# The diagonal of a gated recurrence as two added matmul groups instead of one on the sum of the keys

## The chip, the cores and the metric

The kernel runs on one core of a Trainium2 chip. The metric is the time of one execution on the device in microseconds (us). Below, TensorE is PE, VectorE DVE, ScalarE ACT, GpSimd POOL, and SyncE, which here only issues transfers, SP.

## The reference, cut to what matters

Two transformer blocks run one after the other on 256 tokens of width 2048. Everything here is in the first block, in its recurrent half: eight heads of a bidirectional gated recurrence (HGRN2), with 128 keys per head.

```python
def _hgrn2_direction(q, f_logit, v, lb):
    f = lb + (1.0 - lb) * jax.nn.sigmoid(f_logit)
    return _gla_chunkwise(q, 1.0 - f, v, jnp.log(f))    # the key is k = 1 - f
...
    # in _gla_chunkwise: S_t = diag(f_t) S_{t-1} + k_t v_t^T ; o_t = S_t^T q_t
    a = jnp.einsum('bhtd,bhsd,bhtsd->bhts', q_, k_, jnp.exp(rel))   # rel = b_t - b_s, s <= t
...
    o_fwd = _hgrn2_direction(q, ff, v, lb_fwd)
    o_bwd = jnp.flip(_hgrn2_direction(jnp.flip(q, 1), jnp.flip(fb, 1), jnp.flip(v, 1), lb_bwd), 1)
    o = _rmsnorm(o_fwd + o_bwd, norm_g)
```

At s = t the decay is exp(0) = 1. The diagonal of the summed forward and backward matrix is therefore q·kf + q·kb, which is also q·(kf + kb).

## The kernel before, in words

The kernel is written by hand, with its own semaphores. Each engine follows one list of instructions in order. The list is built from **phases**; a phase is a row of weight chunks of 512 KB. Each chunk goes through four slots: SP loads it into `w_raw` (L663), ACT rounds it to `w_hi` (L1270, L1267), DVE forms the remainder `w_lo` = `w_raw` - `w_hi` (L1742), and PE multiplies both with the activations. SP loads a chunk into a slot once the remainder of the chunk four before it is formed. ACT rounds a chunk once PE has used the chunk four before it. A finished panel of four chunks is moved out of PSUM by an ACT copy (L1291) and a DVE add (L1846).

All other work hangs on the chunks by number: the function `beside` of each engine says what it does after chunk j of a phase. Among it are the pieces of the modulation matrix `w_mod` (512 KB each, loaded by SP at L673, multiplied on DVE at L1809 and L1812).

The phases that matter are, in order:

- `in_f`, 48 chunks: forget gates forward and backward (`hf`, `hb`) and queries (`hq`). Beside them run the attention heads, and the keys `kf` = 1 - `hf`, `kb` = 1 - `hb` on DVE after chunks 37 and 42 (L2313). After chunk 44 DVE forms `qb` = `kf` + `kb` (L2317), which uses the buffer of the later backward queries.
- `in_hg`, 16 chunks, and `w_oa`, 32 smaller ones: beside them runs the recurrence, `hgrn_step(g)`, with g counting the chunks of `in_hg` and on through `w_oa`.

The recurrence is worked out in levels. After chunk 2 of `in_hg` PE runs `diagonal()` (L1097): for each of the 8 heads and 2 halves, four 32x32 blocks of keys times queries, 128 matmuls in all, into PSUM bank 4. It waits for the last panel of `in_f` (the queries), for `mods_done` to reach 8, and for the sum of the keys. `mods_done` reaches 8 by `take_mods(6, 5)` (L2201), the first thing that DVE does in its `hgrn_step(4)`. ACT copies bank 4 to `a_near` (L1626); the entries off the diagonal are replaced later by the levels.

DVE then waits for `diagonal()` and forms `qb` = `hq`·`hb` (L2324) and `hq` = `hq`·`hf` in place (L2326). The first level needs both. Ten steps follow, two (forward, backward) for each of the levels 1, 2, 4, 8 and 16: PE runs 128 matmuls (L1146) after chunks 4 to 13; DVE, after chunks 7 to 16, takes the result with a predicated copy (L2373) and updates queries, keys and gates (L2388, L2391, L2395). A PE step waits for the DVE update of the level before. Two wide levels (L1159), the part off the diagonal (L1170) and the outputs (L1179) follow in `w_oa`.

The matmuls of `diagonal()` and of the levels are small, and PE gets two instructions for each: a weight load and a matmul. In the last level steps and between them nothing loops: the list is unrolled.

Of the kernel before, what the change touches and what calls it, by code (L numbers as in the profile page):

```python
# [21 lines left out]
ALU = mybir.AluOpType  # L22
# [3 lines left out]
P = 128  # L26
# [55 lines left out]
STRIP = 32  # L82
STRIPS = P // STRIP
# [109 lines left out]
def build(nc, d, out):  # L193
    ctx = ExitStack()
    with ctx:
# [52 lines left out]
        ps = ctx.enter_context(nc.psum_tensor("ps", [P, 8, 512], F32))  # L248
# [25 lines left out]
        kf = place("kf", [P, HEADS, T], F32, big + 16 * size_tile)  # L274
        kb = place("kb", [P, HEADS, T], F32, big + 24 * size_tile)
        v1_tok = place("v1_tok", [P, 2, HEADS, P], F32, big + 32 * size_tile)
        qb = place("qb", [P, HEADS, T], F32, big + 32 * size_tile)
        hb = place("hb", [P, HEADS, T], F32, big + 40 * size_tile)
# [314 lines left out]
        def added_at(o, half, quarter):  # L593
# [6 lines left out]
        x_loads = sem("x_loads")  # L600
        late_loads = sem("late_loads")
        c_sig, c_silu = map(sem, ("c_sig", "c_silu"))
        lb_diff, lb_sig, f_sig, lb_done, f_done, k_done, ksum_done, q_done = map(
            sem, ("lb_diff", "lb_sig", "f_sig", "lb_done", "f_done", "k_done", "ksum_done", "q_done"))
        diag_mm, diag_moved = map(sem, ("diag_mm", "diag_moved"))
        ho_stat, ln_stat = Count(sem("ho_stat")), Count(sem("ln_stat"))
        level_mm, level_selected, level_updated, level_placed, off_mm, off_moved = map(
# [147 lines left out]
        def _(pe):  # L755
# [341 lines left out]
            def diagonal():  # L1097
                pe.wait_ge(summed, summed_all("in_f"))
                pe.wait_ge(mods_done, 8)
                pe.wait_ge(ksum_done, 1)  # L1100
                for u in range(2 * HEADS):
                    h, half = divmod(u, 2)
                    for strip in range(STRIPS):
                        cut = slice(half * P + strip * STRIP, half * P + (strip + 1) * STRIP)
                        mm = pe.matmul(ps[strip * STRIP:(strip + 1) * STRIP, 4, u * STRIP:(u + 1) * STRIP],
                                       qb[:, h, cut], hq[:, h, cut], start=True, stop=True)
                mm.then_inc(diag_mm, 1)

            def hgrn_step(g):
# [616 lines left out]
        def _(dve):  # L1726
# [467 lines left out]
            def take_mods(before, bank):  # L2194

                dve.wait_ge(mod_mm, before + 2)
                at_ = 8 * before
                turned = ps[:, bank, :].rearrange("p (i j s) -> p j i s", j=STRIPS, s=STRIP)[:, :, :, 0]
                to, less = (c.rearrange("p (j i) -> p j i", j=STRIPS)
                            for c in (mods[:, at_:at_ + DT], column("b_mod", at_, DT)))  # L2200
                dve.tensor_tensor(to, turned, less, ALU.add).then_inc(mods_done, 2)  # L2201
                dve.wait_ge(mods_done, before + 2)
# [94 lines left out]
            def forget_step(j):  # L2297

                if j == 29:
                    for i, name in enumerate(("hgrn_lb_logits_fwd", "hgrn_lb_logits_bwd")):  # L2300
                        dve.tensor_tensor(lb[:, 2 * i, :], column(name, 0, HEADS), column(name, HEADS, HEADS),
                                          ALU.subtract).then_inc(lb_diff, 1)
                if j == 33:
                    dve.wait_ge(lb_sig, 2)
                    for i in range(2):
                        dve.tensor_scalar(lb[:, 2 * i + 1, :], lb[:, 2 * i, :], -1.0, 1.0, ALU.mult,
                                          ALU.add).then_inc(lb_done, 1)
                if j in (37, 42):
                    i = (37, 42).index(j)
                    if i == 0:  # L2310
                        dve.wait_ge(*att1.out(HEADS))
                    dve.wait_ge(f_done, HEADS * (i + 1))
                    dve.tensor_scalar((kf, kb)[i][:, :, :], (hf, hb)[i][:, :, :], -1.0, 1.0, ALU.mult,  # L2313
                                      ALU.add).then_inc(k_done, 1)
                if j == 44:
                    dve.wait_ge(k_done, 2)
                    dve.tensor_tensor(qb[:, :, :], kf[:, :, :], kb[:, :, :], ALU.add).then_inc(ksum_done, 1)  # L2317

            def hgrn_step(g):

                if g == 4:
                    take_mods(6, 5)
                    dve.wait_ge(diag_mm, 1)
                    dve.tensor_tensor(qb[:, :, :], hq[:, :, :], hb[:, :, :], ALU.mult).then_inc(q_done, 1)  # L2324
                    dve.wait_ge(q_done, 1)
                    dve.tensor_tensor(hq[:, :, :], hq[:, :, :], hf[:, :, :], ALU.mult).then_inc(q_done, 1)  # L2326
                    dve.wait_ge(q_done, 2)
                    dve.wait_ge(diag_moved, 1)
                if 7 <= g < 7 + N_STEPS:
                    level_step(g - 7)  # L2330
                if g in (18, 20):
                    dve.wait_ge(level_mm, N_STEPS + g // 2 - 8)
                    for way in range(2):
                        level_update(g - 8 + way)
                if g == 24:
                    dve.wait_ge(hg_sig, 1)
                    dve.tensor_tensor(hg[:, :, :], hg[:, :, :], hb[:, :, :], ALU.mult).then_inc(hg_gate, 1)
                if g == 26:
                    dve.wait_ge(ho_sum, 1)
                    dve.tensor_scalar(rstd[:, :], ps[:, 4, 0:T], 1.0 / P, EPS, ALU.mult, ALU.add  # L2340
                                      ).then_inc(ho_stat.sem, 1)
                    invert_root(rstd[:, :], ho_stat)
                if g == 29:
                    dve.wait_ge(hg_gate, 1)
                    for i in range(2):
                        heads, banks = slice(4 * i, 4 * i + 4), slice(4 + 2 * i, 6 + 2 * i)
                        dve.wait_ge(ho_sum, 2 + i)
                        dve.scalar_tensor_tensor(qb[:, heads, :], qb[:, heads, :], column("hgrn_norm_g"),
                                                 ps[:, banks, :].rearrange("p b (h t) -> p (b h) t", t=T),
                                                 ALU.mult, ALU.mult).then_inc(h_out, 1)  # L2350
                        dve.wait_ge(h_out, 2 * i + 1)
                        dve.tensor_tensor(qb[:, heads, :], qb[:, heads, :], hg[:, heads, :],
                                          ALU.mult).then_inc(h_out, 1)
                        dve.wait_ge(h_out, 2 * i + 2)
                if g in (30, 31):
                    i = g - 30
                    dve.wait_ge(h_hi, i + 1)
                    tiles = slice(HEADS + 4 * i, HEADS + 4 * i + 4)
                    dve.tensor_tensor(acts[:, tiles, 1, :], qb[:, 4 * i:4 * i + 4, :],
                                      acts[:, tiles, 0, :].bitcast(F32), ALU.subtract).then_inc(h_lo, 1)  # L2360
# [204 lines left out]
```

## Time and profile before

| what | us |
|---|---|
| median of 3 runs | 2661.23 (2660.72 to 2662.78) |
| the profiled execution, its own time | 2660.91 |
| its span in the profile | 2659.0 |
| granted clock of PE, mean over the span | 0.994 of full speed |

The rows in the section after next are from this profiled execution. Times in them count from the start of its span. A row of the timeline gives the start, the duration (of the group when "xN" stands behind it), the engine, the line, the operation with its tiles, and in brackets how long the engine sat idle before it and what ended that. "issue" there means that the engine waited for nothing that the profile shows. Starts and ends of neighbours on one engine overlap by about 0.1 us.

### The profile page before, as it was taken

What the parts mean: (1) busy time and instruction counts of PE and PEld (TensorE: products, weight loads), DVE (VectorE), ACT (ScalarE), POOL (GpSimd) and SP (SyncE); (2) the same over time, 40 slices, a digit from 0 to 9 for tenths busy, and PEclk for the clock granted to TensorE, in tenths of its full rate; (3) what the DMA queues carried; (4) which work ended last, traced back from release to release, by engine and by line L of the source; (5) the groups of instructions that cost most, each with busy time, mean ns of one, the idle gap of its engine ahead of it and who ended that gap; (6) DMA issues with size and microseconds to landing.
All of it is one profiled execution on the core that took longest, in us unless ns stands there. A gap on an engine that the chain in (4) does not pass through costs nothing.

```text
span 2659.0 us, 39728 instructions
## 1 busy us (share of the span) xinstructions
PE 2578.0 (97%) x15041; PEld 2168.5 (82%) x15041; DVE 1829.7 (69%) x2290; ACT 1216.9 (46%) x1562; POOL 58.4 (2%) x83
## 2 busy tenths in 40 slices
PE   6899999989999999999999999999999999999998
PEld 3588777868888888888888888878788888888887
DVE  5778899888864456645648888887666555555444
ACT  4354553464434344444544444465644444444343
POOL 2100000020000000000010000000000000000000
PEclk8999999999999999999999999999999999999999
DMA  9978794858866666565565655556466555566554
GB/s 359 362 256 306 233 344 161 299 185 293 282 206 226 195 188 186 188 197 184 175 212 179 199 175 167 167 180 201 150 198 189 189 187 186 187 189 207 194 193 158
DMA packets 413756, 567.09 MB, mean 213 GB/s; under 512 B 17997, under 2 KB 302066, under 8 KB 412736
## 3 DMA queue, kind: packets, MB, share of 16 engines
q1 hardware_dynamic: 408800, 548.72, 63.2%
q0 software_dynamic: 4832, 16.68, 1.8%
q8 instruction: 83, 1.36, 0.2%
q14 instruction: 41, 0.34, 0.0%
HBM read 563.22 MB, written 2.11 MB: 213 GB/s over the span
## 4 chain that ended last, share of the span: by engine, by line
PE 48%; DVE 2%; ACT 0%; issue 0%; DVEq 0%; ACTq 0%
PE ps L783 22%; PE ps L780 11%; PE ps L802 5%; PE ps L801 5%; PE ps L800 5%; DVE w_lo L1742 1%; PE ps L881 0%; PE ps L903 0%; DVE x_tok L2009 0%; DVE tmp L1849 0%; DVE pr L1829 0%; PE ps L837 0%; DVE ring L2159 0%; ACT pr L1708 0%; DVE pr L1856 0%
## 5 line engine op out<-in xcount | busy, mean ns | idle before, releaser
L1742 DVE TENSOR_TENSOR w_lo<-w_raw,w_hi 128x1024 fp32r<-128x1024 f32 (+1 forms) x870 | 1051.9, 1214 | 670.0 <-ACT w_hi L1267 347.6
L783 PE MATMUL ps<-acts,w_hi 128*128 128x512 f32 x4096 | 1321.7, 398 | 15.9 <-DVE w_lo L1742 7.8
L780 PEld LDWEIGHTS ps<-acts,w_lo 128*128 128x128 f32 x4096 | 769.9, 188 | 169.1 <-issue 1.2
L1270 ACT CAST w_hi<-w_raw 128x1024 fp32r<-128x1024 f32 (+1 forms) x542 | 563.7, 1044 | 647.5 <-PE ps L783 567.9
L780 PE MATMUL ps<-acts,w_lo 128*128 128x256 f32 x4096 | 828.4, 278 | 0.5 <-issue 0.5
L783 PEld LDWEIGHTS ps<-acts,w_hi 128*128 128x128 f32 x4096 | 640.2, 189 | 38.1 <-issue 15.2
L1267 ACT CAST w_hi<-w_raw 128x1024 fp32r<-128x1024 f32 x328 | 339.4, 1040 | 474.1 <-PE ps L802 393.5
L800 PE MATMUL ps<-w_hi,ff 128*128 128x512 f32 x864 | 336.3, 389 | 0.0
L802 PE MATMUL ps<-w_hi,ff 128*128 128x512 f32 x864 | 336.1, 389 | 0.0
L801 PE MATMUL ps<-w_lo,ff 128*128 128x512 f32 x864 | 336.1, 389 | 0.0
L800 PEld LDWEIGHTS ps<-w_hi,ff 128*128 128x128 f32 x864 | 162.2, 188 | 34.5 <-issue 0.8
L801 PEld LDWEIGHTS ps<-w_lo,ff 128*128 128x128 f32 x864 | 162.2, 188 | 33.9
L802 PEld LDWEIGHTS ps<-w_hi,ff 128*128 128x128 f32 x864 | 162.2, 188 | 33.3
L800 PE MATMUL ps<-w_hi,acts 128*128 128x512 f32 (+1 forms) x384 | 152.8, 398 | 4.4 <-DVE w_lo L1742 2.7
L1812 DVE SCALAR_TENSOR_TENSOR mod_acc<-mod_w,silu_c,mod_acc 128x1024 f32<-128x1024 f32 x120 | 151.9, 1277 | 0.0
L801 PE MATMUL ps<-w_lo,acts 128*128 128x512 f32 (+1 forms) x384 | 149.9, 390 | 0.0
L802 PE MATMUL ps<-w_hi,acts 128*128 128x512 f32 (+1 forms) x384 | 149.8, 390 | 0.0
L1829 DVE SCALAR_TENSOR_TENSOR pr<-pr,cols (+15 forms) x240 | 113.9, 475 | 10.9 <-DVE pr L1829 6.0
L1291 ACT COPY half_sum<-ps 128x512 f32<-128x512 f32 x154 | 89.6, 582 | 39.9 <-PE ps L783 39.9
L800 PEld LDWEIGHTS ps<-w_hi,acts 128*128 128x128 f32 x384 | 74.3, 193 | 29.9 <-issue 11.9
L802 PEld LDWEIGHTS ps<-w_hi,acts 128*128 128x128 f32 x384 | 74.2, 193 | 14.4
L801 PEld LDWEIGHTS ps<-w_lo,acts 128*128 128x128 f32 x384 | 74.4, 194 | 13.6
(331 smaller groups left out, 1542.1 us busy)
## 6 DMA issues: line engine op xcount, KB each, us to landing
w_raw<-in_w_in SPq DMA_DIRECT2D x216, 512.0 KB, 3.9
w_raw<-in_w_down SPq DMA_DIRECT2D x216, 512.0 KB, 4.5
w_raw<-in_w_gate_up SPq DMA_DIRECT2D x176, 512.0 KB, 3.6
mod_w<-in_w_mod SPq DMA_DIRECT2D x160, 512.0 KB, 6.3
w_raw<-in_w_up SPq DMA_DIRECT2D x128, 512.0 KB, 4.2
w_raw<-in_w_out SPq DMA_DIRECT2D x64, 512.0 KB, 4.7
mod_more<-in_w_mod SPq DMA_DIRECT2D x32, 512.0 KB, 12.0
w_raw<-in_w_in POOLq DMA_DIRECT2D x16, 512.0 KB, 7.2
```

What stands on the lines that cost most here:

```text
L780: mm = pe.matmul(ps[:, bank, 0:T], w_lo[:, slot, k, c:c + P], lin_.act[:, kk, 0, :], start=False, stop=at_last and n == 0, skip_group_chec ...
L783: mm = pe.matmul(ps[:, bank, :], w_hi[:, slot, k, c:c + P], lin_.act[:, kk, :, :], start=at_first, stop=at_last and n == 1, skip_group_che ...
L800: pe.matmul(o, a_hi, hi, start=at_first, stop=False, skip_group_check=True)
L801: pe.matmul(o, a_hi, lo, start=False, stop=False, skip_group_check=True)
L802: mm = pe.matmul(o, a_lo, hi, start=False, stop=at_last, skip_group_check=True)
L1267: act.copy(wide[1][:, slot, 0:kn, 0:lin_.width], wide[0][:, slot, 0:kn, 0:lin_.width]).then_inc(hi_ready, 1)
L1270: act.copy(w_hi[:, slot, 0:kn, 0:lin_.width], w_raw[:, slot, 0:kn, 0:lin_.width]).then_inc(hi_ready, 1)
L1291: act.copy(half_sum[:, pair, 0:n, :], ps[:, 2 * pair:2 * pair + n, T:2 * T]).then_inc(half_ready, 1)
L1742: dve.tensor_tensor(low[cut], raw[cut], high[cut].bitcast(F32), ALU.subtract).then_inc(lo_ready, 1)
L1812: ins = dve.scalar_tensor_tensor(acc, mod_w[:, slot, :], c, acc, ALU.mult, ALU.add)
L1829: ins = dve.scalar_tensor_tensor(o, z_, w, o, ALU.mult, ALU.add)
```

## The change

DVE's sum of the keys (L2317) and its semaphore go. PE forms the diagonal by two matmuls that add up in PSUM, of forward and of backward keys, so it runs 256 small matmuls instead of 128, and waits for the keys (`k_done`) instead of their sum. As `qb` no longer holds the sum, DVE forms the backward queries' product before it waits for `diagonal()`.

```diff
@@ diagonal(), PE
-                pe.wait_ge(ksum_done, 1)
+                pe.wait_ge(k_done, 2)
                 for u in range(2 * HEADS):
                     h, half = divmod(u, 2)
-                    for strip in range(STRIPS):
-                        cut = slice(half * P + strip * STRIP, half * P + (strip + 1) * STRIP)
-                        mm = pe.matmul(ps[strip * STRIP:(strip + 1) * STRIP, 4, u * STRIP:(u + 1) * STRIP],
-                                       qb[:, h, cut], hq[:, h, cut], start=True, stop=True)
+                    for way, k_ in enumerate((kf, kb)):
+                        for strip in range(STRIPS):
+                            cut = slice(half * P + strip * STRIP, half * P + (strip + 1) * STRIP)
+                            mm = pe.matmul(ps[strip * STRIP:(strip + 1) * STRIP, 4, u * STRIP:(u + 1) * STRIP],
+                                           k_[:, h, cut], hq[:, h, cut], start=way == 0, stop=way == 1,
+                                           skip_group_check=True)
                 mm.then_inc(diag_mm, 1)
@@ forget_step(j), DVE
-                if j == 44:
-                    dve.wait_ge(k_done, 2)
-                    dve.tensor_tensor(qb[:, :, :], kf[:, :, :], kb[:, :, :], ALU.add).then_inc(ksum_done, 1)
@@ hgrn_step(g), DVE
                 if g == 4:
                     take_mods(6, 5)
+                    dve.tensor_tensor(qb[:, :, :], hq[:, :, :], hb[:, :, :], ALU.mult).then_inc(q_done, 1)
                     dve.wait_ge(diag_mm, 1)
-                    dve.tensor_tensor(qb[:, :, :], hq[:, :, :], hb[:, :, :], ALU.mult).then_inc(q_done, 1)
-                    dve.wait_ge(q_done, 1)
                     dve.tensor_tensor(hq[:, :, :], hq[:, :, :], hf[:, :, :], ALU.mult).then_inc(q_done, 1)
                     dve.wait_ge(q_done, 2)
                     dve.wait_ge(diag_moved, 1)
```

## Rows read from the trace of the kernel before

**Rows 1.** The page: busy time by engine.
```profile
PE 2578.0 (97%) x15041; PEld 2168.5 (82%) x15041; DVE 1829.7 (69%) x2290; ACT 1216.9 (46%) x1562; POOL 58.4 (2%) x83
```
**Rows 2.** Busy time by window: PE, PEld, DVE, ACT, POOL, clock, DMA share, GB/s.
```profile
370.00:380.00 10.00, 8.60 (x50) 7.26 (x49) 10.00 (x9) 4.68 (x5) 0.00 (x0) 1.00 1.05 358
...
400.00:410.00 10.00, 8.62 (x291) 7.24 (x282) 9.96 (x11) 2.02 (x2) 0.00 (x0) 1.00 0.52 159
...
460.00:470.00 10.00, 8.85 (x57) 7.62 (x55) 9.93 (x12) 4.49 (x6) 0.00 (x0) 1.00 0.38 122
```
**Rows 3.** The timeline, the last chunks of `in_f`, around the sum of the keys.
```profile
368.11 1.05 ACT L1270 CAST w_hi<-w_raw 128x1024 fp32r<-128x1024 f32 x1 [1.82 <-DMA w_raw<-in_w_in]
369.39 2.28 DVE L2317 TENSOR_TENSOR qb<-kf,kb 128x2048 f32<-128x2048 f32 x1
371.59 1.22 DVE L1742 TENSOR_TENSOR w_lo<-w_raw,w_hi 128x1024 fp32r<-128x1024 f32 x1
372.86 0.50 PE L783 MATMUL ps<-acts,w_hi 128*128 128x512 f32 x1 [1.40 <-DVE w_lo L1742]
```
**Rows 4.** The timeline of ACT and DVE, up to the modulation that `diagonal()` waits for.
```profile
383.53 1.05 ACT L1270 CAST w_hi<-w_raw 128x1024 fp32r<-128x1024 f32 x1 [1.91 <-DMA w_raw<-in_w_in]
384.61 1.23 DVE L1742 TENSOR_TENSOR w_lo<-w_raw,w_hi 128x1024 fp32r<-128x1024 f32 x1 [1.73 <-ACT w_hi L1270]
391.20 0.17 DVE L2201 TENSOR_TENSOR mods<-ps,cols 128x16 f32<-128x16 f32 x1
```
**Rows 5.** The timeline of PE: `diagonal()`, then chunks 3 and 4.
```profile
391.47 1.29 PE L1105 MATMUL ps<-hq,qb 128*32 128x32 f32 x128
392.69 0.50 PE L783 MATMUL ps<-acts,w_hi 128*128 128x512 f32 x1
...
397.93 0.73 PE L783 MATMUL ps<-acts,w_hi 128*128 128x512 f32 x2 [1.02 <-issue]
```
**Rows 6.** The timeline of PE: the first two level steps.
```profile
399.75 1.19 PE L1146 MATMUL ps<-hq,kf 128*32 128x16 f32 x118
401.47 0.27 PE L1146 MATMUL ps<-hq,kf 128*32 128x16 f32 x10 [0.54 <-issue]
...
404.68 1.05 PE L1146 MATMUL ps<-qb,kb 128*32 128x16 f32 x102
406.57 0.40 PE L1146 MATMUL ps<-qb,kb 128*32 128x16 f32 x26 [0.84 <-issue]
```
**Rows 7.** The timeline of DVE: the two products, and the first two level steps.
```profile
392.87 2.29 DVE L2324 TENSOR_TENSOR qb<-hq,hb 128x2048 f32<-128x2048 f32 x1 [1.50 <-PE ps L1105]
395.19 2.29 DVE L2326 TENSOR_TENSOR hq<-hq,hf 128x2048 f32<-128x2048 f32 x1
397.52 1.23 DVE L1742 TENSOR_TENSOR w_lo<-w_raw,w_hi 128x1024 fp32r<-128x1024 f32 x1
403.32 0.73 DVE L2373 COPY_PREDICATED ring<-masks,ps 128x256 f32<-128x256 uint8 x1
...
409.14 0.73 DVE L2373 COPY_PREDICATED ring<-masks,ps 128x256 f32<-128x256 uint8 x1
```
**Rows 8.** The waits of PE, 450 to 480 us.
```profile
PE ps L1170 <- DVE hb L2395: 1.1, 1, 1.1
```
**Rows 9.** The DMA queues: whole span, then 0.25 us from 395.25 and from 399.0.
```profile
q8 instruction: 83, 1.36, 0.2%
...
q8 instruction: 1, 0.02, 29.1%
...
q8 instruction: 1, 0.02, 26.0%
```
**Rows 10.** Windows of 1 us, columns as in rows 2.
```profile
394.00:395.00 1.00, 1.00 (x7) 0.87 (x7) 1.00 (x1) 1.00 (x2) 0.00 (x0) 1.00 1.10 380
...
398.00:399.00 1.00, 1.00 (x6) 0.87 (x7) 1.00 (x2) 0.00 (x0) 0.00 (x0) 1.00 0.00 0
...
401.00:402.00 1.00, 0.53 (x11) 0.47 (x11) 1.00 (x2) 0.00 (x0) 0.00 (x0) 1.00 0.88 307
```

More of the change, by code:

```diff
@@ L602, in build @@
         c_sig, c_silu = map(sem, ("c_sig", "c_silu"))
-        lb_diff, lb_sig, f_sig, lb_done, f_done, k_done, ksum_done, q_done = map(
-            sem, ("lb_diff", "lb_sig", "f_sig", "lb_done", "f_done", "k_done", "ksum_done", "q_done"))
+        lb_diff, lb_sig, f_sig, lb_done, f_done, k_done, q_done = map(
+            sem, ("lb_diff", "lb_sig", "f_sig", "lb_done", "f_done", "k_done", "q_done"))
         diag_mm, diag_moved = map(sem, ("diag_mm", "diag_moved"))
```

## The prediction

> **What bounds the kernel now.** I read the page first: PE is busy 97% of the span [rows 1], so a change can only move the end through PE's idle time or PE's work. The windows around the edit show where PE idles and who is full. In the last chunks of `in_f` the DMA engines are full (share 1.05) and DVE too; through the recurrence DVE is full in each of the seven windows from 400 to 470 us, of which the first and the last stand here, while PE has gaps and the DMA share falls to 0.38 [rows 2]. From DVE's timeline: after its wait of 1.50 us for `diagonal()` it has no gap until 473 us. At the end of the stretch PE's off-diagonal matmuls wait 1.1 us for DVE's last update [rows 8]. So from 393 to 466 us DVE's list sets the time, and what DVE gains or loses there reaches the end, as all later loads and matmuls follow from it. The third view is PE's idle time marked "issue": it stops three times for nothing a semaphore explains, for 1.02, 0.54 and 0.84 us, twice in the middle of a run of 128 small matmuls [rows 5, 6].
>
> **The stops are instruction loading.** Between the releases at 397.93 and 401.47 PE issues the last 9 matmuls of chunk 4 and 118 of the first level step. Each is a weight load and a matmul, so that is 254 instructions, and two waits make 256. Between 401.47 and 406.57 it issues 10 + 16 + 102 = 128 matmuls, again 256 [rows 6]. The queue q8 moves 1.36 MB in 83 packets, 16.4 KB each, which is 256 instructions of 64 bytes; a packet moves at 395.25 and one at 399.0, some 2.5 us before the release at 397.93 and the one at 401.47 [rows 5, 6, 9]. I read it so: PE holds the block that it works on and one more, and asks for the next when it enters a block. From entry to the next block's arrival it took 3.54 us from 397.93 to 401.47, with the DMA engines idle at first, and 5.10 us from 401.47 to 406.57, with a share of 0.88 [rows 6, 10]. The stop at 397.93 has a boundary 23 matmuls after `diagonal()`; 256 instructions earlier, less 46 and about three waits, lies 104 matmuls before the end of `diagonal()`, so after its 24th. At 9.5 ns each (1.22 us from its start to the next line's, by 128) that is 391.70. This block came 6.23 us after it was asked for, with the DMA engines full (1.10) until about 396 [rows 5, 10].
>
> **The parts of the change. The sum of the keys goes.** It takes 2.28 us of DVE. Behind it waits the remainder at 371.59, whose rounded chunk was there at 368.11 + 1.05 = 369.16; PE waits 1.40 us for it [rows 3]. Without the sum it starts at 369.4 and ends at 370.6, before PE is done with the chunk before (371.46). PE gains 1.40 us here, and next it needs nothing late until `diagonal()`.
>
> **That gain is lost at the diagonal.** `diagonal()` starts at 391.47, right behind DVE's `take_mods` at 391.20 + 0.17, which it waits for. That instruction ends a chain which goes back to the remainder at 384.61, held 1.73 us by ACT's rounding, held 1.91 us by a landing [rows 4, 5]. The landings come as the full DMA engines let them, so earlier requests do not bring them forward; at most the 358 GB/s of the window from 370 rise to the 380 that the engines reach at 394, 6% of the 13.5 us between, or 0.8 us [rows 2, 10]. I take 0, as the engines are full in either case (1.05 and 1.10). PE arrives 1.4 us early and waits.
>
> **The second product on PE.** 128 more matmuls of the same shape at 9.5 ns are 1.22 us. With no stop, DVE's in-place product would start at 392.87 + 1.22 = 394.09 instead of 395.19, as `qb` is formed at 391.4 to 393.7, in the old wait: 1.10 us gained [rows 5, 7].
>
> **The stop it brings.** The change adds 256 instructions within `diagonal()`: one block. The boundary after 24 matmuls stays at 391.70 and asks for the next block then. That block is needed 128 matmuls later, at 392.92, where before it was needed at 396.91 (and was late by 1.02). Bounds: it may come after 3.54 us (395.24) or after 6.23 (397.93), or PE may hold more blocks and not stop. I take 397.93, since the request falls at the same time into the same full DMA engines. Then 104 matmuls remain: chunk 3 starts at 397.93 + 0.99 = 398.92 instead of 392.69 (+6.23), and DVE's product at 399.10 instead of 395.19: **+3.9 us on DVE**. ACT's copy of bank 4 and two roundings stand behind the same wait, but are done by 401.5, in time for DVE's next remainder at 401.4.
>
> By the Trainium skill, "Runtime: NRT & Kernel Launch", section "Instruction fetch mechanics", blocks are of 256 instructions, but PE holds 2048 of them and loading is hidden behind issue; by that the stop would not come and DVE would gain the 1.10 us. The trace agrees with the block and not with the hiding. The sum does without this page.
>
> **The first level step.** The boundary in chunk 4 is reached at 396.91 + 6.23 = 403.14 without its old stop, and asks for the next block. The boundary in the level step is 3.0 us on, at 406.1. The block takes 3.54 us in a quiet queue and 5.10 in a busy one; before, this request met idle engines (share 0.00 at 398), now it comes just behind the remainder of chunk 5 (397.52 + 3.9 + 1.2 = 402.6), which lets new loads go [rows 7, 10]. I take 4.3, the middle: 407.44. The last 10 matmuls take 0.27 us and DVE starts 0.11 us after PE's end, as at 392.87 for an end at 391.47 + 1.29; so DVE can use the step at 407.82 (before: 401.85). DVE itself would be there at 403.32 + 3.9 = 407.2. So its shift grows to **+4.5 us**. With 3.54 it stays 3.9, with 5.10 it is 5.3. The second step does not hold DVE again: its block comes by 407.44 + 5.10 = 412.54 and its end is at 413.05 with the 0.40 and 0.11 us behind, while DVE has 5.82 us of its own work between the two uses (403.32 to 409.14), so it comes at 413.6 [rows 6, 7].
>
> Chain: +4.5 us on DVE from 408 us, no gap in which it could be won back, on to the off-diagonal matmuls and the end. The profiled execution took 2660.91 and would take 2665.4; its 0.32 us to the median leave 2665.7.
>
> **Rivals.**
> 1. *A shorter load.* The block in `diagonal()` comes after 3.54 us, at 395.24: DVE's product starts at 395.24 + 0.99 + 0.18 = 396.41, +1.2 us: 2662.4. For it: the quiet loads. Against: the same request took 6.23.
> 2. *No stop.* PE holds enough instructions, or the stops were something else. Then DVE gains 1.1 us; but PE is 1.22 us later at the first level step, which DVE could take from 401.85 + 1.22 = 403.07 against 403.32: a gain of only 0.25 us if the old stops stay, 1.1 if they go: 2661.0 to 2660.1. For it: no stop shows within 128 matmuls of `diagonal()` itself. This is also what the page of the Trainium skill would give. Against: three stops at a spacing of 256 instructions.
> 3. *Slower by more than 0.2%.* The place is the first level step: if the block asked for at 403.14 takes over 5.1 us, DVE loses more than 5.3 us in all. At 6.23 us it comes at 409.37 and DVE goes on at 409.75: +6.4, 2667.6. For it: DVE's late remainders send loads off just before the request. Against: these are few transfers, and 5.10 is the longest in this stretch.
> 4. *The wait is not free.* What the change says of the queries' product holds only while it is formed inside the wait; PE's lead of 1.4 us could shorten that wait if the landings moved by the 0.8 us above. That takes 0.8 us off any of these, and is inside their range.
>
> **How the numbers follow.** A measurement of this kernel can tell about 0.2%, 5.3 us, from no change. Forecast (3.9 to 5.3): 0.50. Rival 1 and values between: 0.18. Rival 2: 0.13. Rival 3 and worse: 0.17. The rest, 0.02, is a gain I do not see. The range from 2660.0 to 2667.7 takes in rivals 1 and 2 and rival 3 at its price. A few hundredths at the forecast's upper edge pass 5.3 us. Faster by over 0.2%: 0.02; within: 0.79; slower: 0.19.
>
> **What would show it.** Right: PE runs from 370 to 390 without the 1.40 wait; its diagonal is split into about 152 and 104 matmuls with an "issue" gap of some 5 us; the product into `hq` starts near 399; the gap in chunk 4 is gone and the first level's grows. Wrong: an unbroken diagonal of 2.5 us, or a split at another count; a start of `diagonal()` well before 391; or DVE idle between 410 and 466, which would give the shift back.

## The result, and the profile after

| | before | after |
|---|---|---|
| median of 12 runs each, side by side | 2663.14 us | 2669.64 us |
| lowest and highest | 2660.72, 2665.50 | 2665.80, 2673.99 |
| ratio of the medians, 95% interval | | 1.0021 [1.0013, 1.0028] |
| the profiled execution | 2660.91 us | 2666.58 us |
| its span | 2659.0 us | 2664.8 us |

The kernel is slower by 0.21%, about 5.6 us by the ratio. The forecast was 2665.7 with a range up to 2667.7, so the time lies above the range. Two errors add up in that. The median of before over 12 runs is 1.9 us above the one of the three runs shown, and the slowdown is some 1 us (by the ratio) or 2 us (by the medians, 6.5) larger than the 4.5 us that were worked out.

The page of the kernel after, busy time by engine, against [rows 1]:

```profile
PE 2583.9 (97%) x15169; PEld 2173.0 (82%) x15169; DVE 1828.7 (69%) x2289; ACT 1216.6 (46%) x1562; POOL 58.4 (2%) x83
...
q8 instruction: 84, 1.38, 0.2%
```

PE has 128 matmuls more and q8 one packet more, as one block of 256 instructions should show. DVE has one instruction less. Its busy time fell by only 1.0 us, although the sum took 2.28.

PE's timeline, the diagonal and the chunk behind it, against [rows 5] (start, duration, engine, line, operation, count, idle time before):

```profile
390.67 0.24 PE L1106 MATMUL ps<-hq,kf 128*32 128x32 f32 x5 [2.30 <-issue]
...
392.52 0.31 PE L1106 MATMUL ps<-hq,kf 128*32 128x32 f32 x6
396.76 0.21 PE L1106 MATMUL ps<-hq,kf 128*32 128x32 f32 x1 [3.93 <-issue]
...
398.31 0.80 PE L783 MATMUL ps<-acts,w_hi 128*128 128x512 f32 x1
...
399.33 1.05 PE L783 MATMUL ps<-acts,w_hi 128*128 128x512 f32 x2
```

Two things are to be seen. The diagonal is cut in two: 151 matmuls, counted over all its rows, then 3.93 us of nothing, then 105. And everything in it is slow: the first 151 take 392.83 - 390.67 = 2.16 us. The pair of chunk matmuls at 399.33 takes 1.05 us, where the same pair takes 0.62 at 402.24. The windows say why (columns as in [rows 2]; the clock is the third column from the right):

```profile
388.00:390.00 2.00, 0.37 (x3) 0.05 (x1) 2.00 (x3) 0.00 (x0) 0.00 (x0) 1.00 0.93 330
391.00:392.00 1.00, 1.00 (x93) 1.00 (x86) 1.00 (x1) 0.00 (x0) 0.00 (x0) 0.50 1.00 395
395.00:396.00 1.00, 0.00 (x0) 0.00 (x0) 0.00 (x0) 0.00 (x0) 0.00 (x0) 0.50 0.11 30
400.00:401.00 1.00, 1.00 (x4) 0.85 (x4) 0.97 (x2) 0.93 (x1) 0.00 (x0) 0.50 0.00 0
401.00:402.00 1.00, 1.00 (x6) 0.83 (x5) 1.00 (x2) 0.00 (x0) 0.00 (x0) 0.96 0.00 0
```

PE sat idle for 2.30 us ahead of the diagonal. Then the granted clock was 0.50, the lower level of 1.2 GHz, from about 391 to about 401. Before, it was 1.00 in the windows of [rows 10] and in all those between them.

DVE's timeline, against [rows 7]:

```profile
390.40 0.17 DVE L2203 TENSOR_TENSOR mods<-ps,cols 128x16 f32<-128x16 f32 x1
390.60 2.29 DVE L2322 TENSOR_TENSOR qb<-hq,hb 128x2048 f32<-128x2048 f32 x1
398.45 2.29 DVE L2324 TENSOR_TENSOR hq<-hq,hf 128x2048 f32<-128x2048 f32 x1 [5.56 <-PE ps L1106]
...
407.62 0.74 DVE L2371 COPY_PREDICATED ring<-masks,ps 128x256 f32<-128x256 uint8 x1 [0.96 <-PE ps L1148]
...
449.14 0.44 DVE L2371 COPY_PREDICATED ring<-masks,ps 128x256 f32<-128x256 uint8 x1 [2.33 <-PE ps L1148]
...
460.30 1.23 DVE L2386 TENSOR_TENSOR hq<-hq,hf 128x1024 f32<-128x1024 f32 x1 [1.25 <-PE ps L1161]
```

The backward queries' product does run in the old wait. The in-place product starts 3.26 us later than before (398.45 against 395.19), and the first level step 4.30 later. This execution was itself early: `take_mods` starts at 390.40 against 391.20. Counted from there, the two shifts are 4.06 and 5.10 us. Then come two waits that were not there before. They take the shift from 4.45 us at the eighth step (442.56 against 438.11) to 6.88 at the ninth (449.14 against 442.26) and to 8.2 at 460.

Behind both waits stand stops of PE. Its timeline in the level steps:

```profile
407.29 0.27 PE L1148 MATMUL ps<-hq,kf 128*32 128x16 f32 x10 [0.73 <-issue]
...
429.34 0.95 PE L1148 MATMUL ps<-qb,kb 128*32 128x16 f32 x90 [0.28 <-issue]
...
434.71 1.09 PE L1148 MATMUL ps<-hq,kf 128*32 128x16 f32 x106 [1.13 <-issue]
...
440.09 1.22 PE L1148 MATMUL ps<-qb,kb 128*32 128x16 f32 x122 [1.12 <-issue]
...
444.47 0.40 PE L780 MATMUL ps<-acts,w_lo 128*128 128x256 f32 x2 [2.05 <-issue]
```

Before, PE's stops for "issue" from 407 to 464 us were two:

```profile
435.86 0.39 PE L780 MATMUL ps<-acts,w_lo 128*128 128x256 f32 x2 [0.49 <-issue]
...
440.41 0.30 PE L1146 MATMUL ps<-hq,kf 128*32 128x16 f32 x11 [1.42 <-issue]
```

### The profile page after: what moved, and what is told of

It reads as the page before. It is cut to its first block, busy times and chain, and to the rows that moved or that the text cites. A ratio compares the mean times of both kernels' runs of the same rounds, so it can differ in the third digit from the quotient of the medians.

```text
span 2664.8 us, 39982 instructions
## 1 busy us (share of the span) xinstructions
PE 2583.9 (97%) x15169; PEld 2173.0 (82%) x15169; DVE 1828.7 (69%) x2289; ACT 1216.6 (46%) x1562; POOL 58.4 (2%) x83
## 4 chain that ended last, share of the span: by engine, by line
PE 48%; DVE 3%; ACT 0%; issue 0%; DVEq 0%; ACTq 0%
PE ps L783 22%; PE ps L780 11%; PE ps L802 5%; PE ps L801 5%; PE ps L800 5%; DVE w_lo L1744 1%; PE ps L881 0%; PE ps L903 0%; DVE x_tok L2011 0%; DVE tmp L1851 0%; DVE pr L1831 0%; DVE pr L1858 0%; PE ps L837 0%; DVE ring L2161 0%; ACT pr L1710 0%
```

## The experiments

The theory: 128 more matmuls are 256 more instructions, one block, and PE stops until that block has come. The rivals are that the cost lies in adding into PSUM, in the wait for the modulation, in the fallen clock, or in the product that DVE moved. Each run below is beside the kernel before on the same chip.

**twice_sum.** The kernel before, with its one product issued twice. Nothing is added up, DVE's order is the old one.

```diff
-                    for strip in range(STRIPS):
+                    for strip in (*range(STRIPS), *range(STRIPS)):
```

> The kernel before with its one product of the keys' sum simply issued twice over (256 matmuls, nothing adds up, the sum stays on DVE, the queries' product stays behind the wait). Theory of instruction loading: the diagonal stops for 3 to 5 us after some 150 matmuls, DVE's two products start that much later, and as both lie behind the wait the time is 5 to 8 us above before. Rival, the price is that of the added matmuls or of adding up in PSUM: no stop, 1.2 us more at most.

Measured: 2671.98 against 2663.70, ratio 1.0034 [1.0023, 1.0045]. PE's timeline, then DVE's:

```profile
392.87 1.48 PE L1105 MATMUL ps<-hq,qb 128*32 128x32 f32 x151
399.46 1.62 PE L1105 MATMUL ps<-hq,qb 128*32 128x32 f32 x105 [5.11 <-issue]
```

```profile
401.22 2.29 DVE L2324 TENSOR_TENSOR qb<-hq,hb 128x2048 f32<-128x2048 f32 x1 [8.50 <-PE ps L1105]
```

The same cut, 151 and 105, and a stop of 5.11 us. So the 128 matmuls more are enough for the stop, and neither the adding up nor the second operand is needed. The loss, 8.3 us by the medians and 9.1 by the ratio, is a little more than expected. At the full clock the 151 matmuls take 1.48 us here, against 2.16 in the kernel after.

**one_way.** The kernel after, with one way of the two, so the backward keys' part of the diagonal is missing.

```diff
-                    for way, k_ in enumerate((kf, kb)):
+                    for way, k_ in enumerate((kf,)):
...
-                                           k_[:, h, cut], hq[:, h, cut], start=way == 0, stop=way == 1,
+                                           k_[:, h, cut], hq[:, h, cut], start=True, stop=True,
```

> The changed kernel with the forward keys' product alone (128 matmuls; the backward keys' part of the diagonal is left out of the result). All that the change does on DVE stays. Loading: no stop in the diagonal, stops as in the kernel before it, 0.5 to 2.5 us faster than before. Rival, PE's early arrival and its idle time before the diagonal lower the clock and that costs by itself: slower than before by 1 us or more, with a granted clock of 0.5 after the diagonal.

Measured: 2663.00 against 2663.70, 0.9997 [0.9988, 1.0006].

```profile
391.90 1.29 PE L1106 MATMUL ps<-hq,kf 128*32 128x32 f32 x128 [2.33 <-issue]
```

The diagonal is in one piece again, and the loss is gone with it. The gain of 0.5 us or more that was expected does not show. PE's idle time ahead of it is that of the kernel after (2.33 us against 2.30), but here the clock stays at 1.00.

**old_order.** The kernel after, with the backward product put back behind the wait.

```diff
-                    dve.tensor_tensor(qb[:, :, :], hq[:, :, :], hb[:, :, :], ALU.mult).then_inc(q_done, 1)
                     dve.wait_ge(diag_mm, 1)
+                    dve.tensor_tensor(qb[:, :, :], hq[:, :, :], hb[:, :, :], ALU.mult).then_inc(q_done, 1)
```

> The changed kernel with the backward queries' product put back behind the wait for the diagonal. Loading: PE's late blocks bound the recurrence, so 2.3 us more of DVE behind the wait cost 0 to 1.5 us over the changed kernel. Rival, DVE alone bounds the recurrence: 2.3 us over the changed kernel.

Measured: 2668.42 against 2663.70, 1.0021 [1.0012, 1.0030], the ratio of the kernel after. DVE is 3.8 us later at the first level step than in the kernel after (411.42 against 407.62), yet they reach the product that applies the gate at 487.60 and 487.73. Of the 3.8 us, 1.7 are there already at `take_mods` (392.06 against 390.40). So no worth shows of the part of the change that was meant to save time on DVE; the intervals of the two ratios would hide 2 us or more.

**own_buffer.** The opposite: the kernel before, with the keys' sum in memory of its own, so that the backward product needs no wait. PE has its 128 matmuls.

```diff
+        ksum = place("ksum", [P, HEADS, T], F32, x_at)
...
-                                       qb[:, h, cut], hq[:, h, cut], start=True, stop=True)
+                                       ksum[:, h, cut], hq[:, h, cut], start=True, stop=True)
...
-                    dve.tensor_tensor(qb[:, :, :], kf[:, :, :], kb[:, :, :], ALU.add).then_inc(ksum_done, 1)
+                    dve.tensor_tensor(ksum[:, :, :], kf[:, :, :], kb[:, :, :], ALU.add).then_inc(ksum_done, 1)
...
-                    dve.wait_ge(diag_mm, 1)
                     dve.tensor_tensor(qb[:, :, :], hq[:, :, :], hb[:, :, :], ALU.mult).then_inc(q_done, 1)
-                    dve.wait_ge(q_done, 1)
+                    dve.wait_ge(diag_mm, 1)
```

> The kernel before with the keys' sum in a buffer of its own, so that one product of 128 matmuls is enough and the backward queries' product still lies ahead of the wait. Loading: no stop in the diagonal; DVE's in-place product starts at 393.7 instead of 395.2; 0.5 to 1.5 us faster than before. Rival, the moved product is what costs: slower than before, as the changed kernel.

Measured: 2664.40 against 2663.70, 1.0003 [0.9994, 1.0012]. This one missed: no gain. The in-place product starts at 393.88, 1.31 us earlier than before. DVE's timeline shows where that goes:

```profile
403.32 0.73 DVE L2373 COPY_PREDICATED ring<-masks,ps 128x256 f32<-128x256 uint8 x1 [1.23 <-PE ps L1147]
...
444.79 0.43 DVE L2373 COPY_PREDICATED ring<-masks,ps 128x256 f32<-128x256 uint8 x1 [2.30 <-PE ps L1147]
```

The first level step starts at 403.32, to the hundredth where it started before. DVE comes early and waits 1.23 us for PE, then 2.30 at the ninth step. The reading "from 393 to 466 us DVE's list sets the time" held only because DVE came as late as PE's blocks.

**no_mods_wait and own_buffer_nw.** The kernel after, and own_buffer, without the diagonal's wait for the modulation, which its operands don't need.

```diff
                 pe.wait_ge(summed, summed_all("in_f"))
-                pe.wait_ge(mods_done, 8)
```

> The changed kernel without PE's wait for the modulation ahead of the diagonal. PE is free at 388.4 and starts at once, so it does not idle for 2.3 us, and asks for the block 2.1 us earlier. Loading with a fixed delay: released at 394.7, the products 2 us earlier than in the changed kernel. Loading held up by the full DMA engines until they drain at 395: released at 396.7 as before, a gap of over 6 us, no gain but for the clock. In both the granted clock is 1.0 when the diagonal begins. Time 0 to 2.5 us below the changed kernel. Rival, the added products' arithmetic is the price: no gap once the wait is gone, 4 us below the changed kernel or more.

> The keys' sum in its own buffer, one product, the queries' product ahead of the wait, and no wait of PE for the modulation: DVE never waits for the diagonal and PE keeps its lead. If blocks bound the recurrence, as the gaps in the levels say, PE's 2.5 us earlier start moves the whole chain: 1 to 3 us below the kernel before. If DVE alone bounds it: 1.5 us below. If something later takes it back: no change.

Measured: no_mods_wait 2667.49 against 2664.35, 1.0015 [1.0006, 1.0025]; own_buffer_nw 2664.57 against 2664.35, 1.0005 [0.9996, 1.0014]. No_mods_wait starts its diagonal at 390.32 at the full clock and is cut after 151 matmuls all the same:

```profile
396.49 0.21 PE L1105 MATMUL ps<-hq,kf 128*32 128x32 f32 x1 [4.69 <-issue]
```

```profile
395.00:396.00 1.00, 0.00 (x0) 0.00 (x0) 0.00 (x0) 0.00 (x0) 0.00 (x0) 0.50 1.09 358
```

So the wait does not make the stop, and by the ratio it is not the main cost either. Here the clock falls inside the stop, at about 395. Own_buffer_nw is a second miss: 1 to 3 us less than before were expected. In it, the level steps show what binds them; each of these rows is the release of a block:

```profile
419.62 0.82 PE L1146 MATMUL ps<-hq,kf 128*32 128x16 f32 x74 [0.67 <-issue]
424.72 0.95 PE L1146 MATMUL ps<-qb,kb 128*32 128x16 f32 x90 [0.83 <-issue]
429.82 1.09 PE L1146 MATMUL ps<-hq,kf 128*32 128x16 f32 x106 [0.84 <-issue]
434.92 1.22 PE L1146 MATMUL ps<-qb,kb 128*32 128x16 f32 x122 [0.85 <-issue]
```

They stand exactly 5.10 us and 128 matmuls apart. I read it so: the next block is asked for when PE enters this one, and comes 5.10 us later, so PE cannot go faster, whatever DVE does. Half_levels below tests it.

**split.** No_mods_wait with the first half of the units issued one chunk earlier, after the first chunk of `in_hg`, so that the instructions are not all used up in one burst.

```diff
-            def diagonal():
+            def diagonal(part):
...
-                for u in range(2 * HEADS):
+                for u in range(HEADS * part, HEADS * (part + 1)):
...
+                    diagonal(0)
                 if g == 2:
-                    diagonal()
+                    diagonal(1)
```

> The same with the diagonal in two halves of 128 matmuls, the first after chunk 1, the second after chunk 2. The same 256 matmuls, but a chunk of 2.8 us lies between them, so a block lasts about 4 us instead of 1.3. Loading: the one gap of 4 to 5 us falls to 2 us or less, the clock stays at 1.0, 3 to 6 us below the changed kernel, within 2 us of the kernel before. Rival, arithmetic or adding up in PSUM: as slow as the changed kernel.

Measured: 2665.71 against 2664.35, 1.0010 [1.0001, 1.0019]. The diagonal has no gap and the clock stays at 1.00 through it. The stops are now in chunk 4 and in the first level step:

```profile
399.15 0.28 PE L780 MATMUL ps<-acts,w_lo 128*128 128x256 f32 x1 [1.77 <-issue]
...
404.07 0.30 PE L1149 MATMUL ps<-hq,kf 128*32 128x16 f32 x10 [1.89 <-issue]
```

By the ratio the loss is half that of the kernel after, about the smallest gain that was expected, but the interval overlaps that of no_mods_wait (1.0006 to 1.0025). The extra block still has to come.

**warm.** The kernel after, with PE kept busy by matmuls on constants while it waits for the modulation.

```diff
                 pe.wait_ge(summed, summed_all("in_f"))
+                keep_warm(7, 8)
                 pe.wait_ge(mods_done, 8)
```

> The changed kernel with eight 128x256 matmuls of constants into an idle bank ahead of the wait for the modulation, so that PE does not idle for 2.3 us before the diagonal. Theory, the clock fell because of that idle time: the first part of the diagonal runs at 9.5 ns for each matmul instead of 13, the gap of 4 to 5 us stays, and the clock falls late in the gap or not at all; 0.5 to 2 us below the changed kernel. Rival, the gap alone costs: the same as the changed kernel within 0.5 us.

Measured: 2667.67 against 2663.60, 1.0017 [1.0008, 1.0026].

```profile
390.40 3.62 PE L979 MATMUL ps<-consts 128*128 128x256 f32 x16
...
396.66 0.19 PE L1107 MATMUL ps<-hq,kf 128*32 128x32 f32 x1 [1.37 <-issue]
```

The granted clock stays at 1.00 and the DVE product starts 0.52 us earlier (397.93). The cut comes after 135 matmuls, 16 earlier than in the kernel after: the profile counts the warm matmuls as 16, and they stand ahead in the same list. So what is counted is PE's instructions, and not the matmuls of the diagonal. The release comes at 396.66, only 2.7 us after the first matmul of the diagonal, at 393.94, and no other load took less than 3.5. So the block was not asked for when the matmuls ran. It fits that PE's sequencer had issued ahead, behind the warm matmuls still running, but no view shows the request itself. As PE's list waits for the end of `take_mods` at 392.48, this block took 4.2 us at most, if the request keeps to that wait. The ratio is 0.0004 lower, which is inside the intervals. By this pair the fallen clock costs about half a microsecond of the time before the levels and is not the main loss. `take_mods` started 1.9 us later here (392.31 against 390.40), so the half microsecond is no more than an estimate.

**fewer_pieces.** The kernel after, with four of the six modulation pieces beside `in_hg` left out, which fill the DMA engines in this phase. The result lacks their part. It ran once.

```diff
-            Phase("in_hg", 1, [(l_g, i, 0) for i in range(4)], sides(scale_m[0:6], range(1, 7))),
+            Phase("in_hg", 1, [(l_g, i, 0) for i in range(4)], sides(scale_m[0:2], range(1, 3))),
```

> The changed kernel with four of the six modulation pieces beside the next phase left out (their part of the MLP scale is missing from the result), so that the DMA engines have less in their queues when the diagonal starts, and DVE less to do ahead of it. Loading held up by full DMA engines: the block's packet goes 1 to 2 us after the request and the gap in the diagonal falls from 3.9 us to 2.0 to 2.8. Loading with a fixed delay: the gap stays at 3.9 or above. DVE has 5 us less, so the whole time says nothing.

```profile
395.82 0.19 PE L1106 MATMUL ps<-hq,kf 128*32 128x32 f32 x1 [3.96 <-issue]
```

Also a miss. The stop stays at 3.96 us. From the request, 24 matmuls into the diagonal, to the release it takes 5.2 us, against 5.9 in no_mods_wait (both at the full clock when they ask, the request reckoned at 9.5 ns each: 390.39 and 390.32, plus 0.23). The DMA share was 0.37 to 0.91 in the windows from 390 to 394 us and 0.87 to 1.10 there. So with less full DMA engines the delay is 0.7 us shorter, and kernels with all transfers differ among themselves by as much. Reckoned alike, the block took 6.4 us in twice_sum and 6.8 in old_order, whose stop was the longest:

```profile
399.32 0.21 PE L1106 MATMUL ps<-hq,kf 128*32 128x32 f32 x1 [5.53 <-issue]
```

Empty engines were not tried. The single time, 2670.27, says nothing beyond that.

**half_levels.** Own_buffer_nw, with half of the matmuls in the level steps from the fifth on (the third level), so that a part of the recurrence is missing.

```diff
-                for u in range(2 * HEADS):
+                for u in range(2 * HEADS if n < 2 else HEADS):
```

> The kernel with the keys' sum in its own buffer and no wait for the modulation, with the matmuls of heads 4 to 7 left out in the level steps 4 to 9 (their part of the recurrence is missing), so that each of these steps has 128 instructions fewer. DVE's work is the same. If blocks bound these steps, DVE's waits of 2.1 and 1.5 us vanish and the time falls by 2.5 to 4 us against that kernel and below the kernel before by 2 to 4. If DVE bounds them: the same time.

Measured: 2660.18 against 2663.60, 0.9987 [0.9978, 0.9995]. DVE's waits from 391 to 470 us, first in own_buffer_nw, then in half_levels (engine, line, what it waited for: total, times, longest):

```profile
DVE ring L2372 <- PE ps L1146: 2.1, 1, 2.1
DVE hq L2387 <- PE ps L1159: 1.5, 1, 1.5
```

```profile
DVE ring L2372 <- PE ps L1146: 1.7, 1, 1.7
```

The one wait left in half_levels is that of the first level step, which is whole. Those of the late steps are gone, and DVE applies the gate 3.6 us earlier (479.18 against 482.75). Of these 3.6 us, 1.4 are there already at `take_mods` (390.81 against 392.22). With the instructions halved DVE sets the pace, with all of them PE does. The halving also saves PE 0.5 us of matmuls in each step (0.74 us for 64, 1.27 for 128), so it doesn't part the blocks from the matmuls' own time. For the blocks speak PE's stops for "issue": in own_buffer_nw 6.4 us from 419 to 444 us, in half_levels 0.58.

**thin and thin_early.** If instructions are the price, the diagonal can be had for few. DVE multiplies the keys' sum by the queries element by element. Both kernels stand on own_buffer_nw. PE adds over the partitions with four matmuls of 512 columns against a column block of ones, which the profile counts as 8, in the place of 128.

```diff
-                for u in range(2 * HEADS):
...
-                        mm = pe.matmul(ps[strip * STRIP:(strip + 1) * STRIP, 4, u * STRIP:(u + 1) * STRIP],
-                                       qb[:, h, cut], hq[:, h, cut], start=True, stop=True)
+                units = ksum[:].rearrange("p h (half s t) -> p (h half) s t", half=2, t=STRIP)
+                for strip in range(STRIPS):
+                    mm = pe.matmul(ps[strip * STRIP:(strip + 1) * STRIP, 4, :].rearrange("p (u t) -> p u t", t=STRIP),
+                                   ones[:, 0:STRIP], units[:, :, strip, :], start=True, stop=True)
...
-                if g == 2:
+                if g == 3:
                     diagonal()
...
-                    dve.wait_ge(diag_mm, 1)
+                    dve.tensor_tensor(ksum[:, :, :], hq[:, :, :], ksum[:, :, :], ALU.mult).then_inc(ksum_done, 1)
```

Thin does that product all at step 4. Thin_early does heads 0 to 5 in the remainder ahead of chunk 3 of `in_hg`, where DVE used to wait, and the last two heads at step 4.

> The diagonal without the many small matmuls: DVE multiplies the queries with the keys' sum (2.3 us more on DVE) and PE sums over the keys by 4 matmuls of 512 columns with ones, so PE has one block of instructions fewer than the kernel before and DVE waits for no diagonal. If blocks bound the recurrence: its gaps move earlier by up to 4 us and the time is 0 to 2 us below the kernel before, in spite of DVE's 0.8 us more. If DVE bounds it: 0.8 us above before. By either 5 us or more below the changed kernel.

> The thin diagonal with three quarters of its product (heads 0 to 5) formed where DVE idles for a load at the start of the next phase, so that only 0.6 us of it is left ahead of the two products. DVE's in-place product starts 1.7 us earlier than in the thin kernel, at about 393.6. If DVE bounds the levels now that PE has a block fewer: DVE has no wait up to 450 us and the time is 1 to 2 us below the thin kernel and 1.5 to 3.5 us below the kernel before. If the blocks take it back, as with the sum in its own buffer: the same as the thin kernel, with DVE waits of 2 us at a level step.

Measured: thin 2662.35 against 2663.60, 0.9996 [0.9986, 1.0007]; thin_early 2659.47 against 2663.84, 0.9984 [0.9975, 0.9993]. DVE's timeline of thin_early:

```profile
382.28 1.75 DVE L1740 TENSOR_TENSOR ksum<-hq,ksum 128x1536 f32<-128x1536 f32 x1
...
390.91 0.69 DVE L2325 TENSOR_TENSOR ksum<-hq,ksum 128x512 f32<-128x512 f32 x1
...
393.72 2.29 DVE L2328 TENSOR_TENSOR hq<-hq,hf 128x2048 f32<-128x2048 f32 x1
```

PE has 120 matmuls fewer than before and stops only twice between 398 and 462 us, for 0.71 and 1.94 us. DVE still waits 1.2 us for PE, at the first wide level. Thin_early computes what the reference asks for and is faster than both kernels: by 0.16% than the one before.

**Where the shift goes after the levels.** Each row is the profiled execution of a kernel. It gives the shift of DVE's gate product against before's 479.50, the shift of that execution's time against 2660.91, and the shift of the medians.

| kernel | gate | its time | medians |
|---|---|---|---|
| after | +8.2 | +5.7 | +6.5 |
| twice_sum | +8.4 | +6.5 | +8.3 |
| old_order | +8.1 | +8.6 | +4.7 |
| warm | +7.5 | +9.1 | +4.1 |
| split | +5.3 | +4.8 | +1.4 |
| own_buffer | +3.9 | +3.5 | +0.7 |
| one_way | +3.9 | +5.6 | -0.7 |
| no_mods_wait | +3.6 | +3.0 | +3.1 |
| own_buffer_nw | +3.3 | +4.4 | +0.2 |
| thin_early | +0.2 | +0.7 | -4.4 |
| thin | +0.1 | +2.4 | -1.3 |
| half_levels | -0.3 | -0.7 | -3.4 |

With fewer_pieces (+7.3, +9.4), the time less the gate shift lies between -2.6 and +2.3 us in the 13 executions, with a mean of +0.3. So a shift at 480 us passes to the end in full, give or take 2.5 us that differ from one execution to the next. The 2.5 us that the kernel after seems to win back are within this scatter.

The gate shifts hold scatter too. DVE's keys `kb`, which lie ahead of every change and are alike in all fourteen executions, do not start at one time. They start between 360.33 and 363.22; the first and the last of these rows are the extremes, the kernel after and twice_sum, and the middle one is before:

```profile
360.33 1.22 DVE L2315 TENSOR_SCALAR kb<-hb 128x2048 f32<-128x2048 f32 x1
```

```profile
361.80 1.22 DVE L2313 TENSOR_SCALAR kb<-hb 128x2048 f32<-128x2048 f32 x1
```

```profile
363.22 1.22 DVE L2313 TENSOR_SCALAR kb<-hb 128x2048 f32<-128x2048 f32 x1
```

The medians lie on average 2.7 us below the gate shifts (12 kernels, from 0.1 to 4.6). The profiled execution of before is below the medians of before by 2.2 us (2663.14, its own 12 runs) to 3.4 (2664.35). It was a lucky one, and shifts read against its trace are on average some 2.7 us too large. The record bounds where the luck lay. At `kb` this execution is no earlier than the others (361.80, their mean is 361.84), and behind the gate only 0.3 us is left, so most of it lies between. One_way, own_buffer and own_buffer_nw have before's number of small matmuls and before's median, and in each DVE waits 3.6 to 4.8 us in all for PE's level steps from 391 to 470 us. In the execution of before it waits only for the diagonal. I infer that before's typical execution has some of these waits; with one trace of it this is not shown.

## Why the prediction missed

**The base: too low.** The range was hung on the median of three runs, 2661.23. Twelve runs give 2663.14. That is 1.9 of the 3.9 us between the forecast and the time.

**The cause: right.** One block of 256 instructions, asked for 24 matmuls into the diagonal and missing 128 later: forecast a cut at about 152 and 104, it came at 151 and 105. Twice_sum shows it without any of the change's arithmetic, and warm shows that the cut moves with the instructions ahead of it. Of the Trainium skill's "Runtime: NRT & Kernel Launch", section "Instruction fetch mechanics", the blocks agree; that loading is hidden by issue does not, as the stops of 3.93, 4.69, 5.11 and 5.53 us show. Rival 2 is out.

**The sum goes, PE comes early: right, and priced wrong.** The 1.40 us wait is gone, and PE waits 2.30 us at the diagonal for the modulation. The diagonal begins at 390.67, 0.80 us before the old start. That looks like rival 4 and is not: the execution was 1.47 us early at `kb` already, ahead of the change, and from there `take_mods` comes 0.7 us later than before. "PE arrives 1.4 us early and waits" had no price. Behind this idle time, at about 391 and ahead of the stop, the clock fell to 0.50 for 10 us. That costs 2.16 - 1.48 = 0.68 us in the first 151 matmuls, hidden by the stop, and 1.69 us from the release to DVE's start in the place of 1.17. Chunk 3 takes 1.3 us longer (from its first to its last matmul 3.93 us instead of 2.66), beside DVE's own work.

**"I take 397.93": 1.2 us too late.** The release came at 396.76. The block was asked for 24 x 12.8 ns = 0.31 us after 390.67, so at 390.98, not at 391.70, and took 5.8 us where I took 6.2. Rival 1, 3.54 us, is out. The slower clock behind it takes back about half: DVE's product comes at 398.45, forecast 399.10.

**The first level step: the right number, with luck in it.** Forecast 407.82 and +4.5 us; it came at 407.62 and +4.3, after a DVE wait of 0.96, and the release at 407.29 (forecast 407.44). Two errors cancel in that. PE reached the boundary at about 403.8 and not at 403.14, as chunk 3 ran at the slower clock, and the block took about 3.5 us and not 4.3. And the whole execution was 0.8 us early: counted from `take_mods` the shift is 5.1.

**"No gap in which it could be won back, on to the end": this step failed.** It asked only whether DVE could win time and not whether it could lose more: whether PE's blocks come in time for DVE was checked for the first two level steps and no further, and of PE's five stops for "issue" before (391 to 464 us), the prediction names three. The two at 435.86 and 440.41 are missing. In their place the run showed DVE waiting for PE: it lost 2.4 us at the ninth level step and 1.3 at 460, so the shift went from 4.3 us to 8.2. The rival that names further loss put it at the first level step, and it fell later. The blocks end at the same instructions before and after: 10 and 26 matmuls ahead of a step's end in [rows 6] and in the kernel after, and the stops at 435.86 and 444.47 are at one place in the list. Only the time of arrival differs. Before, at the sixth to the eighth step, PE waited for DVE and not for a block (0.78, 0.17 and 0.71 us). From 429.34 to 434.71 and on to 440.09 a block took 5.4 us, where a step of DVE takes 5.1 us there and then 4.5 and 4.1 (433.95, 438.42, 442.56), so PE falls behind with each until DVE stands. At 445.7 the clock fell once more, as in the window

```profile
446.00:448.00 2.00, 2.00 (x64) 1.47 (x67) 0.80 (x1) 0.64 (x1) 0.00 (x0) 0.50 0.09 20
```

This second fall of the clock is not what makes the wait: DVE waits 2.06 to 2.30 us at the same step in own_buffer, own_buffer_nw and one_way, at a clock of 1.00 from 436 to 452 us.

Less the 2.7 us by which before's trace flatters, the loss of 4.3 us at the first level plus 3.9 later is 5.5 us, near the 5.6 of the ratio. That is an estimate: the scatter above is as large as its parts, and the profiled execution of the kernel after was itself 3.1 us below its median.

**"DVE's list sets the time": half right.** Two bounds lie within 1 or 2 us of each other there, DVE's list and PE's blocks. A loss on either shows at the end. A gain on one alone does not, which fits that own_buffer, one_way and own_buffer_nw gained nothing and that old_order shows no loss against the kernel after.

**Still open.** What makes a block take 3.5 us once, 5.1 in the levels and 5.8 to 6.8 here (in warm 4.2 at most) is not settled: thinning out the transfers took off 0.7 us in one execution. The traces say which part varies. In eight loads (two of before, and that of the diagonal in six kernels) the packet shows on q8 2.3 to 2.6 us ahead of the release; in the kernel after at 394.35 for the release at 396.76. From the reckoned request to the packet it took 1.2 us behind 397.93 with idle DMA engines, 2.8 in fewer_pieces, and 3.4 to 4.3 with full ones. That fits a packet that waits behind other transfers. Warm does not fit: there it was 1.7 us at most, with a DMA share of 0.99 to 1.12. So it stays open. That the late blocks of the level steps meet weight transfers was not tried.

## What to carry to other kernels

Count the instructions of an edit as well as their time. Here small matmuls ate a block of 256 in 1.2 us, and the next block needed 3.5 to 6.8 us, so a few wide matmuls are worth work on another engine (120 matmuls fewer and one DVE product more gave 0.16%). Before pricing a gain on the engine that is full, ask which bound stands next to it and how far off it is. Take the base from many runs. Before you read a shift between two traces, compare an instruction ahead of the change, and see how each execution stands to its median.

## What the runs showed of the hardware

The cut after 151 matmuls follows from the number of instructions: it is the same with one operand or two, with and without the wait for the modulation, and 16 matmuls ahead of it move it to 135. 256 instructions used up in 1.2 us (1.6 in the kernel after, at the lower clock) made PE stand for 3.9 to 5.5 us.

The same idle time of PE (2.30 and 2.33 us) ahead of the diagonal was followed by the lower clock in the kernel after and not in one_way. Why it fell in one and not in the other is open.

The times of single executions of one kernel spread over 4 to 13 us (2665.80 to 2673.99 for the kernel after, 2656.83 to 2670.20 for thin), as much as the whole effect or more. Traces of single executions are no finer: an instruction that is alike in all kernels started over a range of 2.9 us at 360 us. What they show is where an engine stood, and for how long.
